# A depthwise convolution moved from VectorE to TensorE as banded products, in a one-core decoder kernel

## The reference

```python
xn = rmsnorm(x, norm_g)
h = xn @ w_in                                   # one projection to all head groups
u = ua * sigmoid(ub)                            # 512 channels
# causal depthwise convolution, 31 taps per channel, then LayerNorm over the 512 channels
y = conv(u_ext, w) + b                          # u_ext: 30 rows of context (zeros, or state_conv for a sample)
yn = (y - mean(y)) * rsqrt(var(y) + 1e-5) * ln_g + ln_b
conv_y = silu(yn)
# attention: each query keeps its top 256 keys by an indexer's score, softmax with a position bias
mix = concat([conv_y * silu(gc), attn_o * silu(ga)])
out = rmsnorm(x + mix @ w_out, final_norm_g)
```

## Time and profile before

| | us |
|---|---|
| median of 3 runs (lowest, highest) | 1969.9 (1963.02, 1970.94) |
| the profiled execution | 1962.63 |
| its span, first to last instruction | 1961.0 |
| PE busy in the span | 1531.0 (78%) |
| DVE busy | 1391.0 (71%) |
| ACT busy | 717.5 (37%) |
| POOL busy | 408.1 (21%) |
| mean granted TensorE clock | 0.895 of full |

### The profile page before, as it was taken

The page is one execution under the profiler, slowest core; times in us unless marked ns, Lnnn a source line. Parts: engine busy times, 40 slices in busy tenths (PEclk is TensorE's granted clock), DMA queues, the critical chain, the costliest instruction groups (busy, mean ns, idle before and its releaser), DMA issues. The chain is left out here.

```text
span 1961.0 us, 26785 instructions
## 1 busy us (share of the span) xinstructions
PE 1531.0 (78%) x9511; PEld 1286.7 (66%) x9511; DVE 1391.0 (71%) x2411; ACT 717.5 (37%) x1256; POOL 408.1 (21%) x297
## 2 busy tenths in 40 slices
PE   5879959799559949692768897888888767369998
PEld 5876959799449949592455565555666545247776
DVE  3413988988888898886259998988789997134442
ACT  3424411332133222230214554555445444244441
POOL 2120314234204313241300000010000111232211
PEclk9989979999779969896768998999899997579999
DMA  7632452223256302221511110110102111613332
GB/s 237 211 72 49 89 100 68 65 64 88 65 195 141 90 34 78 75 59 36 163 55 48 39 54 1 53 53 29 51 28 76 37 48 61 204 62 118 126 128 107
DMA packets 166187, 164.60 MB, mean 84 GB/s; under 512 B 54666, under 2 KB 137618, under 8 KB 166047
## 3 DMA queue, kind: packets, MB, share of 16 engines
q1 hardware_dynamic: 165031, 160.80, 27.8%
q0 software_dynamic: 1024, 2.10, 0.3%
HBM read 100.94 MB, written 57.93 MB: 81 GB/s over the span
## 5 line engine op out<-in xcount | busy, mean ns | idle before, releaser
L661 PE MATMUL psum<-xh,wh 128*128 128x384 f32 (+1 forms) x1056 | 347.2, 329 | 35.0 <-POOL wl L549 32.6
L1248 DVE SCALAR_TENSOR_TENSOR cy<-cu,cw,cy 128x1088 f32<-128x1088 f32 x240 | 354.6, 1477 | 15.6 <-issue 0.4
L661 PE MATMUL psum<-xl,wh 128*128 128x384 f32 (+1 forms) x1056 | 346.3, 328 | 0.0
L661 PE MATMUL psum<-xh,wl 128*128 128x384 f32 (+1 forms) x1056 | 346.3, 328 | 0.0
L1151 ACT ACTIVATE pts<-psT 128x512 f32<-128x512 f32 (+1 forms) x302 | 168.1, 573 | 321.1 <-PE psT L1418 299.0
L661 PEld LDWEIGHTS psum<-xh,wh 128*128 128x128 f32 x1056 | 199.7, 189 | 36.8 <-issue 21.2
L1410 PE MATMUL psU<-kh,qt 128*128 128x512 f32 (+3 forms) x320 | 139.4, 437 | 97.5 <-DVE mx L1302 96.3
L1434 PE MATMUL psO<-pts,vs 128*64 128x128 f32 x2176 | 185.2, 292 | 24.2 <-ACT pts L1151 24.2
L661 PEld LDWEIGHTS psum<-xl,wh 128*128 128x128 f32 x1056 | 199.8, 189 | 0.0
L661 PEld LDWEIGHTS psum<-xh,wl 128*128 128x128 f32 x1056 | 199.6, 189 | 0.0
L777 DVE TENSOR_SCALAR_CACHE_REDUCE hit<-scores,T 128x2064 bf16<-128x2064 f32 (+14 forms) x120 | 184.6, 1538 | 11.0
(11 more groups left out here) (272 smaller groups left out, 2502.2 us busy)
## 6 DMA issues: line engine op xcount, KB each, us to landing
wst<-in_w_in SPq DMA_DIRECT2D x28, 512.0 KB
wst<-in_w_in SPq DMA_DIRECT2D x32, 256.0 KB
qt<-d_q SPq DMA_DIRECT2D x16, 512.0 KB, 4.0
xst<-in_x_prompt SPq DMA_DIRECT2D x15, 512.0 KB, 3.9
xr<-in_x_prompt SPq DMA_DIRECT2D x15, 512.0 KB, 4.6
out_y_prompt<-fin SPq DMA_DIRECT2D x15, 512.0 KB, 3.0
gate<-d_ga SPq DMA_DIRECT2D x17, 256.0 KB, 4.4
d_mix<-mix SPq DMA_DIRECT2D x17, 256.0 KB, 2.2
```

Of the source, the lines that this page charges most:

```text
L661: last = nc.tensor.matmul(u[:, 0:k * P], a[:, w % 2, cc, :], x[:, s0:s0 + k, cc, :], start=(cc == 0 and e == 0), stop=(cc == KC - 1 and e ...
L1248: V.scalar_tensor_tensor(y, u[:, k:k + HALFW], w, y, ALU.mult, ALU.add)
```

## The change

**Stage 2.** `u` is also transposed: 24 jobs `uT`, one per `ua` block, each placed behind the next projection, of three or two PE transposes (68 in all), a copy by ACT into `ut`, and a DMA to `d_un`, which holds for each of 8 groups of 64 channels: 128 token rows, 18 tile slots (slot 0 is the zero context), 64 channels. `d_cw` gets the taps with zeros around them (96 rows per group).

**Stage 3.** DVE's taps go. Tokens are cut in windows of 32: 65 for the prompt and 8 for the samples, 73 in all. For each channel a product with 64 rows (32 of context, 32 of its own; row 0 carries the bias through a row of ones) and a 32 column band matrix gives 32 outputs of each window. 512 such products stand in 20 jobs after steps 1, 2, 2, 3, 3, then 5, 6, 6, 7, 7, then 9 to 11 and 13 to 15. Their operands (`ht`, the bands; `uw`, the windows) are loaded for a quarter of the channels at a time; the buffers are single, so the next quarter's 18 DMAs are issued when the last product of this quarter is done. ACT copies results to `yc`. From step 17 on the normalisation runs in `yc` for one to two tiles per four steps: sum (DVE), mean (PE), subtraction (DVE), squares (POOL), sum (DVE), variance (PE), inverse root (POOL), scaling (DVE), and one transposing product per 32 tokens into channel order (PE, 64 of them and 9 for tile 16), from which ACT and a DMA fill `d_y`.

**Stage 4.** Stages `a` and `b`, the sample convolution and its transposes go; `c` remains. The channels now stand in another order on the partitions, so the gate and `w_out` are loaded by four DMAs of 32 rows where one was. All `w_high` copies follow stage `c` of block 0.

```diff
 select_jobs:
+                jobs.append(("proj", h, c, b))
+                put_late()
+                if name == "ua":
+                    late.append(("uT", h, j, b))
 attend_and_convolve:
+CONV_JOBS = [(q, a, min(BANKA, QA - a)) for q in range(NQ) for a in range(0, QA, BANKA)]
+CONV_STEPS = [(1, 2, 2, 3, 3), (5, 6, 6, 7, 7), (9, 10, 10, 11, 11), (13, 14, 14, 15, 15)]
+SUM_STEP = [17 + 4 * k for k in range(len(NORM))]
...
+            def load_windows(q):
+                if q:
+                    sp.wait_ge(pe_pt, last_conv(q - 1))
+                else:
+                    sp.wait_ge(uw_ones, 1)
+                main = WPT * LAST
+                for r in range(2):
+                    b = 2 * q + r
+                    a0, a1, a2 = CB * r, CB * r + WIN, CB * r + WROWS
+                    u = t.d_un[b].rearrange("p s c -> p (s c)")
+                    sp.dma_start(ht[a0 + 1:a2, :, :].rearrange("p m c -> p (m c)"),
+                                 bass.AP(t.d_cw.tensor, (b * HROWS + 1) * CB, [[CB, WROWS - 1], [1, WIN * CB]])).then_inc(ht_in, 16)
...
+                    sp.dma_start(uw[a1:a2, 0:main, :].rearrange("p (w i) c -> p w (i c)", w=WPT),
+                                 u[:, CB:(LAST + 1) * CB].rearrange("(w p) x -> p w x", p=WIN)).then_inc(uw_in, 16)
...
+                    sp.dma_start(uw[a0 + 1:a1, LAST:main, :].rearrange("p (w i) c -> p w (i c)", w=WPT - 1),
+                                 u[0:P - WIN, CB:(LAST + 1) * CB].rearrange("(w p) x -> p w x", p=WIN)[1:]).then_inc(uw_in, 16)
+                    sp.dma_start(uw[a0 + 1:a1, 0:LAST, :].rearrange("p i c -> p (i c)"),
+                                 u[P - WIN + 1:P, 0:LAST * CB]).then_inc(uw_in, 16)
...
             for p in range(NP_ + 3):
+                for q in range(NQ - 1):
+                    if p == CONV_STEPS[q][-1] + 1:
+                        load_windows(q + 1)
...
-                for tap in range(dtaps[p], dtaps[p + 1]):
-                    conv_tap(tap)
+                for k in range(len(NORM)):
+                    if TURN_STEP[k] == p:
+                        normalise(k)
+                    if SQ_STEP[k] == p:
+                        square_sums(k)
+                    if SUM_STEP[k] + 2 == p:
+                        subtract_mean(k)
+                    if SUM_STEP[k] == p:
+                        sums(k)
...
+            def convolve(e, q, a, k):
+                pt = take_pt(("C", e))
+                if a == 0:
+                    pe.wait_ge(ht_in, 64 * (q + 1))
+                    pe.wait_ge(uw_in, 224 * (q + 1))
+                for x in range(k):
+                    for g in range(4):
+                        r, c = g // 2, QA * (g % 2) + a + x
+                        last = T.matmul(pt[WIN * g:WIN * g + WIN, x * NW:(x + 1) * NW], ht[64 * r:64 * r + WROWS, :, c],
+                                        uw[64 * r:64 * r + WROWS, :, c], start=True, stop=True,
+                                        tile_position=(64 * r, WIN * g))
 mix_out:
-        stages = [(stage, k) for k in range(2) for stage in "abc"]
-        schedule = stages[:5] + [("tile", LAST)] + stages[5:]
+        schedule = [("c", 0), ("tile", LAST), ("c", 1)]
```

More of the change, by code:

```diff
@@ L90, in constants @@
     at("ones")[:] = 1.0 / C
+    for r in range(128):
+        at("flip")[r, r // WIN * WIN + WIN - 1 - r % WIN] = 1
+        at("avg")[r, r % WIN::WIN] = 1.0 / C
     return c
@@ L372, in select_jobs, with put_late @@
 def select_jobs():
-    jobs = []
+    jobs, late = [], []
+    def put_late():
+        jobs.extend(late)
+        late.clear()
     for h, blocks in enumerate(HALVES):
@@ L381, in select_jobs @@
                 jobs += [("score", i, head, a, n) for i in GROUPS[g] for head in range(IH) for a, n in pieces(i)]
-            jobs += [("proj", h, c, b) for b in range(len(blocks))]
+            for b in range(len(blocks)):
+                jobs.append(("proj", h, c, b))
+                put_late()
+                if name == "ua":
+                    late.append(("uT", h, j, b))
+    put_late()
     return jobs
@@ L534, in _ @@
             sp.wait_ge(r_out, 16)
+            for s in range(2):
+                sp.wait_ge(ut_out[s], 16 * len(ut_jobs[s::2]))
             for k in range(3):
@@ L672, in _ @@
                         last = nc.tensor.matmul(u[:, b0:b0 + bn], q, mem.ikl[:, a + b0:a + b0 + bn], start=False, stop=True)
+                elif job[0] == "uT":
+                    m = stage_of_u[job[1:]]
+                    pe.wait_ge(combined, m + 1)
+                    for e in range(slots(job[1], job[3])[1]):
+                        last = nc.tensor.transpose(u[:, e * P:(e + 1) * P], ust[:, m % 2, e * P:(e + 1) * P], ident)
                 elif job[0] == "we":
@@ L1353, in _ @@
             pe.wait_ge(c_in, 32)
-            pe.wait_ge(cw_in, 16)
-            u = take_u(("cw", 0))
-            for c in range(CC):
-                last = T.transpose(u[:, c * TAPS:(c + 1) * TAPS], cwn[:, c * P:(c + 1) * P], ident[0:TAPS, 0:TAPS])
-            last.then_inc(pe_u, 1)
             pe.wait_ge(s_in, 64)
@@ L1438, in products, with mean_of, turn @@
                 last.then_inc(pe_pv, 1)
+            def convolve(e, q, a, k):
[9 more added lines that the diff above has]
+                                        tile_position=(64 * r, WIN * g))
+                last.then_inc(pe_pt, 1)
+            def mean_of(job, x, n):
+                T.matmul(take_pt(job)[:, 0:n], flip[:, 1, :], x, start=True, stop=True).then_inc(pe_pt, 1)
+            def turn(k, i):
+                pt = take_pt(("Y", k, i))
+                if i == LAST:
+                    T.matmul(pt[:, 0:P], yc[:, NWP - 1, :], flip[:, 0, :], start=True, stop=True)
+                    for s in range(NS):
+                        last = T.matmul(pt[:, P + s * CC:P + (s + 1) * CC], yc[:, NWP + s, :],
+                                        flip[:, 0, 0::WIN], start=True, stop=True)
+                else:
+                    for w in range(WPT):
+                        last = T.matmul(pt[:, w * P:(w + 1) * P], yc[:, w * LAST + i, :], flip[:, 0, :], start=True, stop=True)
+                last.then_inc(pe_pt, 1)
             logits(0)
@@ L1598, in _ @@
                 if c < CC:
-                    sp.dma_start(wst[:, c % WS, :], t.w_out[0, c * P:(c + 1) * P, :]).then_inc(w_ld[c % WS], 32)
+                    for q in range(NQ):
+                        r = P * q + QA * c
+                        sp.dma_start(wst[QA * q:QA * q + QA, c % WS, :], t.w_out[0, r:r + QA, :]).then_inc(w_ld[c % WS], 16)
                 else:
@@ L1827, in _ @@
                     n += 1
-                    continue
-                w = len(BLOCKS[k]) * P
-                if what == "a":
-                    pe.wait_ge(y_in[k % 2], 32 * (k // 2 + 1))
-                    if k == 0:
-                        pe.wait_ge(ys_done, 1)
-                    else:
-                        pe.wait_ge(centred, k)
-                    for c in range(CC):
-                        last = T.matmul(ST[:, 0, 0:w], ones, y[:, k % 2, c, 0:w], start=(c == 0), stop=(c == CC - 1))
-                    last.then_inc(mean_done, 1)
-                elif what == "b":
-                    pe.wait_ge(squared, k + 1)
-                    if k:
-                        pe.wait_ge(std_done, k)
-                    for c in range(CC):
-                        last = T.matmul(ST[:, 1, 0:w], ones, tmp[:, c, 0:w], start=(c == 0), stop=(c == CC - 1))
-                    last.then_inc(var_done, 1)
 class Tensors:
```

434 lines of the change are left out of this document (245 added, 189 removed).

## The result

The changed kernel took 1989.9 us (median of 4 runs, 1985.66 to 1994.8), the kernel before 1966.5 us in the same comparison (4 runs). The ratio is 1.0125, 95% interval [1.009, 1.016]: slower by 23 us. The profiled execution took 1985.66 us with a span of 1984.0. One launch of a later run (2860 us, in the run that loads only the first quarter) stood far above all others and is left out of that run's median.

What follows compares the result with a forecast made beforehand. DVE bounds stage 3 with PE close behind. Against 1962.6 us profiled: taps -82, small products +13, convolution products +56, loads +75, stages 2 and 4 -31, sum +31: 1994 us, median forecast 1996, range 1912 to 2040.

Steps and rivals of the forecast that it cites:

- the likeliest case: Stage 3's first four tiles: one DMA engine's queue for the window loads sets the pace, 1965 to 2025 us; chance 0.60.
- taps gone: Stage 3: removing DVE's taps gains 69 us between landmarks and 13 us by an earlier step 1, together -82 us.
- means, variances, transposing products: Stage 3's norm: some 90 small products on PE at 0.15 us each, +13 us.
- convolution products: Stage 3 on PE: 512 products, 1024 instructions at 0.055 us each, +56 us (21 to 110).
- windows' loads and the clock after: Stage 3: 50 us loads, PE waits 22 us for each later quarter, 3 for quarter 0; lower clock +6; sum +75.
- stage 4: Stage 4: six norm product rounds go, -18 us, and the first product comes earlier, -13 us; together -31.
- PE is late next: Stage 3: without the taps PE becomes the bound, so not all of DVE's 355 us come back.
- the line through the earlier trace: Stage 3: PE's unhindered step times in tiles 14 and 4 give 0.87 us a block, 497 us for 64 steps.
- the like row: L1430's products on PE, nearest to the convolution's: 0.038 us an instruction, 0.042 scaled to 73 columns.
- Rival 2: Convolution products in stage 3: strided operands halve PE's rate, 0.085 to 0.11 us apart, total 2025 to 2050 us; chance 0.15.
- Rival 1: Stage 3's window loads spread or use different engines and are back within two steps: 1919 us; chance 0.17.
- Rival 3: Convolution products in stage 3: array row halves run side by side, 0.021 to 0.03 us, total 1960 to 1970; chance 0.08.

Runs made afterwards that it cites:

- few taps: The kernel before with 29 of the 31 taps of each unit left out (16 instead of 248 run), nothing else changed: 1856.5 us, ratio 0.9465.
- spread loads: The changed kernel with each window-load DMA of 31 rows split into 16 and 15, each of 63 into 48 and 15: 1890.7 us, ratio 0.9643.
- doubling: The changed kernel with spread loads and each convolution product made twice (1024 in place of 512): 1925.2 us.
- the run with larger gaps: The changed kernel, loads unchanged, convolution products later and farther apart, normalisation from step 25 in place of 17: 1973.0 us, ratio 1.0053.
- 128 rows: The changed kernel with spread loads, stage 4's w_out and gate loaded by DMAs of 128 successive rows: 1876.1 us, ratio 0.9521.

## Why the prediction was right, step by step

The direction, the likeliest case and the place (a queue through one DMA engine in stage 3's first four tiles) were right, and 1996 lies 6 us off. But its terms erred by more, in both directions, and that the sum came so close is luck: the taps gave 32 us more than forecast and the products cost 19 less, while the loads cost 30 more, the small products 10 and stage 4 5.

| term | forecast | measured | from |
|---|---|---|---|
| taps gone | -82 | -114 | stage 3 538.1 instead of 633.1 with few taps; step 0 by 18 |
| means, variances, transposing products | +13 | +23 | 598.3 us with spread loads, less 538.1, less 37 |
| convolution products | +56 | +37 | 1024 by 0.036; doubling gave 34.5 |
| windows' loads and the clock after | +75 | +105 | waits 99.0; 6 are left of 703.2 - 598.3 |
| stage 2 | 0 | -2 | stage 3's first product at 929.67, was 932.11 (940.78 with few taps, whose stage 2 is the same: no difference shown) |
| stage 4 | -31 | -26 | 267.0 instead of 293.2 |
| sum | +31 | +23 | spans 1984.0 and 1961.0 |

**The taps.** "PE is late next" held. What failed was the sum of extras on the line through the earlier trace rows: it carried 12 us for the last tiles and 10 us for stretches at the lower clock over from a trace in which PE waited for DVE. With the waits gone the clock is 0.99, and the last three tiles take 36.7 us with few taps, not 47. In all, the stretch holds 9 us beyond the line and the tile ends (538.1 less 497 and 32), not 35. Step 0 gave 18 us, not 13. PE's unhindered pace was right: tile 14 took 56.7 us with few taps, where I had worked out 56.

**The loads.** "50 us a quarter" was 55, and the gaps between the quarters were the 28 us of the forecast (26 to 29), so 26, 27 and 29 us of waiting in place of 22. The larger miss is quarter 0: 17 us instead of 3. Step 1 came 21 us earlier than before (1013.76, not 1034.69), where the forecast had 13, so PE stood there 8 us sooner; and the load (issued from 981.54, there at 1040.62) took 59 us and landed 6 later than the 1035 of the forecast. 3 + 8 + 6 are the 17. That SP's own issues are held up I did not foresee; in the changed kernel it hides under PE's wait, and it became the bound once that wait was moved (the run with larger gaps).

**The products.** 0.036 is the like row's pace, so 0.055 was too careful. Rival 2 was wrong as to size and right as to the mechanism: the stride does halve PE's rate, but from 0.0175 and not from 0.042. L1430's 0.038 was no measure of what such a product takes without a stride; that it lies near the strided pace is chance.

**The small products.** 16 instructions of the turning (1689.02 to 1690.83 us) are 0.113 us apart, and a float32 product is two of them, 0.23 us; I had priced it by transposes, at 0.15. At that pace the 91 products (73 transposing, 18 for means and variances) make 21 of the 23 us.

```profile
1689.02 2.05 PE L1646 MATMUL psT<-flip,yc 128*128 128x128 f32 x16
1690.83 0.42 PE L1592 MATMUL psU<-kh,qt 128*128 128x384 f32 x1
```

**Stage 4.** Behind the first product it took 195.4 us, before 222.4: 27 less, of which 18 are the six rounds of the forecast and 5 waits around the norm's stages; the other 4 are open. The 13 us of the start were cancelled: I saw the fourfold issues on SP, not that loads of 32 rows run at 188 GB/s. With 128 rows PE's wait fell by 13 us (55.9 instead of 69.0). The near hit of this term, -26 for -31, is thus luck too: the start gave nothing and the rest 9 more.

**The rivals.** Rival 1 is what the kernel does once its loads are spread: 1891 us, below the 1919 worked out, since the taps gave more and the products cost less. Rival 3's pace (0.021 to 0.03) didn't occur with the strided windows; contiguous ones are faster still, 0.0175.

## What to carry to other kernels

Before moving work to another engine, count the outermost rows of every DMA that feeds it: 31 rows went through one engine (26 GB/s) and 4 through four, and 16 + 15 rows cost nothing. Work out what the moved engine's clock and waits become when the old bound goes, and take each gain of time into the due times of the loads behind it as well: that step 1 came 8 us sooner than forecast was 8 us more of waiting for the first quarter. A wait that is given more time is not gone if the issue of its load blocks others: look at what the issuing engine has behind it.

## What was unexpected in the hardware

- SP's issues of loads that go through one engine are slow themselves: 4.96 us where 31 rows pass in that time, 46 us for a quarter's 18 DMAs, against 13 us for 28 spread ones. That they wait for room in the queue of that engine is my reading of these numbers.
- PE reads a moving operand of 73 float32 columns at a stride of 256 bytes at half the rate (0.036 and 0.0175 us an instruction); as weights it costs nothing that shows.
- DMAs into 32 partitions with all engines full moved 184 to 188 GB/s, those into 128 partitions 314 to 349.
- The contiguous products of 64 rows by 32 columns follow at 0.0175 us. One with 128 by 128 and 512 columns is 0.38 an instruction, 0.054 scaled to 73 columns. That several run side by side would explain it; no run here shows it.
